# The sparse-attention step of a two-model kernel: its compression between the projection's blocks, scaled probabilities, and outputs by column halves

## The reference

```python
q, kc, vc, ks, vs, kw, vw, g = split(h @ w_in)      # 1024, six of 256, 48 columns
kcmp = silu((windows(rope(kc)) + pe) @ w1) @ w2       # 15 windows of 32 tokens, stride 16
vcmp = the same of vc
o_c = softmax(q @ kcmp) @ vcmp                       # compressed part, 15 keys a group
o_s = softmax(q @ ks) @ vs                           # all 4 blocks are chosen: causal
o_w = softmax(q @ kw) @ vw                           # window 512 > 256: causal
gates = sigmoid(g)
out = (gates[0] * o_c + gates[1] * o_s + gates[2] * o_w) @ w_out
```

## Time and profile before

| | |
|---|---|
| median of 3 runs | 2884.92 us (2884.88 to 2886.07) |
| profiled execution's own time | 2884.84 us |
| its span, first to last instruction | 2883.0 us |
| mean granted TensorE clock | 0.994 |
| PE / DVE / ACT / POOL busy | 98% / 65% / 54% / 5% of the span |
| the NSA step on PE | 1202.9 to 1374.6 us |

### The profile page before, as it was taken

The page is one execution under the profiler, slowest core; times in us unless marked ns, Lnnn a source line. Parts: engine busy times, 40 slices in busy tenths (PEclk is TensorE's granted clock), DMA queues, the critical chain, the costliest instruction groups (busy, mean ns, idle before and its releaser), DMA issues.

```text
span 2883.0 us, 34918 instructions
## 1 busy us (share of the span) xinstructions
PE 2812.2 (98%) x13484; PEld 2303.9 (80%) x13484; DVE 1860.1 (65%) x2728; ACT 1546.0 (54%) x2656; POOL 149.1 (5%) x254
## 2 busy tenths in 40 slices
PE   9999999999999999999999999999999999999998
PEld 7887788888788888878888888788787788787786
DVE  6766776676566677646776766677654754645654
ACT  6546654655665465546655546665444444444442
POOL 1010100000000000000001001100100000000000
PEclk9999999999999999999999999999999999999999
DMA  8664467566446766642566675367663665653652
GB/s 261 223 229 161 141 218 248 183 223 222 161 154 217 243 190 229 215 150 70 187 232 219 216 260 186 103 208 242 229 212 135 200 189 189 227 190 132 190 190 88
DMA packets 358629, 559.41 MB, mean 194 GB/s; under 512 B 14624, under 2 KB 246048, under 8 KB 358208
## 3 DMA queue, kind: packets, MB, share of 16 engines
q1 hardware_dynamic: 350720, 535.02, 55.8%
q0 software_dynamic: 7600, 21.81, 2.2%
q10 hardware_dynamic: 144, 0.36, 0.0%
HBM read 556.03 MB, written 1.10 MB: 193 GB/s over the span
## 4 chain that ended last, share of the span: by engine, by line
PE 92%; DVE 5%; ACT 1%; issue 1%; POOL 1%; DMA 0%; DVEq 0%; ACTq 0%; POOLq 0%
PE ps L660 38%; PE ps L721 26%; PE ps L666 19%; PE ps L630 4%; PE ps L832 1%; PE ps L801 1%; DVE LO L1508 1%; POOL ST L2046 1%; DVE XL L1549 0%; DVE M L1626 0%; PE ps L809 0%; DVE M L1587 0%; PE ps L949 0%; DVE SB L1791 0%; ACT SB L1326 0%
## 5 line engine op out<-in xcount | busy, mean ns | idle before, releaser
L660 PE MATMUL ps<-HI,XH 128*128 128x512 f32 (+1 forms) x2496 | 984.1, 394 | 4.0 <-DVE LO L1508 1.4
L660 PE MATMUL ps<-LO,XH 128*128 128x512 f32 (+1 forms) x2496 | 971.4, 389 | 0.0
L1508 DVE TENSOR_TENSOR LO<-RAW,HI 128x1024 fp32r<-128x1024 f32 x468 | 567.6, 1223 | 335.7 <-ACT HI L1169 332.9
L666 PE MATMUL ps<-HI,XL 128*128 128x512 f32 (+1 forms) x2496 | 769.4, 389 | 0.4
L1513 DVE SCALAR_TENSOR_TENSOR LO<-RAW,GC,HI 128x512 fp32r<-128x512 f32 (+1 forms) x896 | 622.4, 744 | 189.1 <-ACT HI L1176 186.6
L1169 ACT ACTIVATE HI<-RAW 128x1024 fp32r<-128x1024 f32 x468 | 490.5, 1059 | 457.6 <-PE ps L721 286.6
L1176 ACT ACTIVATE HI<-RAW,GC 128x512 fp32r<-128x512 f32 (+1 forms) x896 | 588.1, 714 | 158.0 <-PE ps L666 133.0
L666 PEld LDWEIGHTS ps<-HI,XL 128*128 128x128 f32 x2496 | 466.7, 188 | 105.7 <-DVE XL L1549 7.9
L660 PEld LDWEIGHTS ps<-HI,XH 128*128 128x128 f32 x2496 | 469.9, 188 | 101.2 <-issue 2.4
L660 PEld LDWEIGHTS ps<-LO,XH 128*128 128x128 f32 x2496 | 470.1, 188 | 92.6
L721 PE MATMUL ps<-HI,AH 128*128 128x512 f32 x880 | 273.5, 392 | 0.0
(11 more groups left out here) (182 smaller groups left out, 1968.7 us busy)
## 6 DMA issues: line engine op xcount, KB each, us to landing
RAW<-in_ffn_w_in SPq DMA_DIRECT2D x350, 512.0 KB, 4.7
RAW<-in_ffn_w_out SPq DMA_DIRECT2D x88, 1024.0 KB, 5.0
RAW<-in_w_ada SPq DMA_DIRECT2D x48, 1024.0 KB, 5.1
RAW<-in_w_in SPq DMA_DIRECT2D x44, 1024.0 KB, 5.1
RAW<-in_w_ffn_in SPq DMA_DIRECT2D x88, 512.0 KB, 4.7
RAW<-in_diff_w_in SPq DMA_DIRECT2D x24, 1024.0 KB, 5.1
RAW<-in_w_ffn_out SPq DMA_DIRECT2D x22, 1024.0 KB, 4.9
RAW<-in_moba_w_in SPq DMA_DIRECT2D x12, 1024.0 KB, 5.1
```

The lines of the kernel that those rows point to most:

```text
L660: e.matmul(ps[:, b + t, 0:nw], XH[:, k, t * P:(t + 1) * P], q[s][:, c * nw:(c + 1) * nw], start=(k == 0 and q is HI), stop=False)
L666: i = e.matmul(ps[:, b + t, 0:nw], XL[:, k, t * P:(t + 1) * P], HI[s][:, c * nw:(c + 1) * nw], start=False, stop=(k == 7))
L1508: e.tensor_tensor(LO[n % NSPLIT][:, 0:w], RAW[t.buf][:, at[1] * w:(at[1] + 1) * w], HI[n % NSPLIT][:, 0:w].bitcast(F32), ALU.subtract).the ...
```

## The change

The NSA step alone is rewritten; all others keep their code.

- The projection's blocks come in another order and cut: kc and vc, ks and vs, kw and vw, then the queries in two, each of 512 columns, and the gates' 48. The compression weights are loaded in two pairs of tiles, ahead of blocks 3 and 4.
- The compression runs between the blocks: its first half (`windows(0)`) behind block 2, its second behind block 3, hidden turn and second layer within block 4, the first scores too. The key turns are `doubled(0..3)`, of which two stand behind block 1, one behind block 2 and one in block 3 ahead of k2 = 2. `clock()` is gone. The small block writes to ps[4] and ps[5].
- The gates are made as exp(-x) on ACT, plus one and reciprocal on DVE, in place of a sigmoid.
- A unit is now a pair of heads with its two key sets in turn (units 2p and 2p + 1), and there is one more set of scores in flight ahead of the loop. The probabilities in SB are multiplied with CG, reciprocal sum times gate: one piece of 128 columns by DVE (`weights`), three pieces by POOL. The compressed probabilities are scaled too, in one DVE product.
- The turned heads are copied to PT by ACT (`first_head`) and DVE (`second_head`).
- `outputs_by_columns`: values are the weights, PT moves, and head j goes to partitions 64 j to 64 j + 63, so a pair's outputs stand turned, with rows by head, as XH and XL need them. The pair's two units and its compressed part (`compressed(p)`) add up in one bank; ACT and DVE take XH and XL from it (`pair_high`, `pair_low`). M, TP and `outputs_flipped` are not used here.
- Three of the output projection's halves are split at u = 9, 11 and 13. The last unit's outputs come behind the first row group of the projection.

Core of the diff (comment lines name the engine's queue; lines in brackets stand for several):

```diff
+NSA_BLOCKS = ((1024, 512), (1536, 512), (2048, 512), (0, 512), (512, 512), (2560, 48))
...
+            elif st.kind == "nsa":
+                for n, (c0, nw) in enumerate(NSA_BLOCKS):
+                    if n in (3, 4):
+                        tiles_windows(n - 3, st)
+                    tile_cols(a["nsa_w_in"][st.j], c0, nw, 0, st)
+                    tile_cols(a["nsa_w_in"][st.j], c0, nw, 1, st)
+                tile_rows(a["nsa_w_out"][st.j], st)
...
+            def outputs_by_columns(st, u, b, first, v):
+                PT = st.t["PT"]
+                for kt in range(2):
+                    for j in range(2):
+                        o = e.matmul(ps[64 * j:64 * j + 64, b, kt * P:S], v(kt),
+                                     PT[:, u % 2, j, 0:S] if kt == 0 else PT[:, u % 2, j, S:S + P],
+                                     start=(first and kt == 0), stop=False, skip_group_check=True)
+                o.then_inc(s_mix, 1)
...
 # TensorE
+                first_block(st, 512)
+                later_block(st, 1, 512)
+                doubled(0, 0)
+                doubled(1, 1)
+                later_block(st, 2, 512)
+                doubled(2, 0)
+                e.wait_ge(s_e, 8)
+                windows(0)
+                later_block(st, 3, 512, lambda k2: doubled(3, 1) if k2 == 2 else None)
+                windows(1)
+                later_block(st, 4, 512, in_queries)
+                e.wait_ge(s_tn, c["tn"] + 10)
+                later_block(st, 5, 48, None, 4)
+                e.wait_ge(s_cp, c["cp"] + 5)
+                unit_scores(1)
+                e.wait_ge(s_cp, c["cp"] + 6)
+                queries_turned(5)
+                e.wait_ge(s_ex, c["ex"] + 1)
+                unit_scores(2)
...
+                def in_queries(k2):
+                    if k2 == 1:
+                        hidden_turned()
+                    elif k2 == 2:
+                        queries_turned(4)
+                        compressed_made()
+                    elif k2 == 3:
+                        e.wait_ge(s_tn, c["tn"] + 10)
+                        e.wait_ge(s_cp, c["cp"] + 4)
+                        unit_scores(0)
...
-                e.wait_ge(s_vb, 4)
-                clock()
...
+                for u in range(17):
+                    if 1 <= u < 14:
+                        e.wait_ge(s_ex, c["ex"] + u + 1)
+                        unit_scores(u + 2)
+                    if u >= 1:
+                        turned(u - 1)
+                    if u >= 2:
+                        mixed(u - 2)
+                    if u in (2, 3):
+                        compressed_turned(u - 2)
...
+                def ready(k, t):
+                    if (k, t) == (0, 0):
+                        e.wait_ge(s_pt, c["pt"] + 15)
+                        e.wait_ge(s_p1, c["p1"] + 15)
+                        e.wait_ge(s_ol, c["ol"] + 4)
+                    elif (k, t) == (0, 1):
+                        e.wait_ge(s_ol, c["ol"] + 8)
...
 # ScalarE
+                block_out(0)
+                split(st.w0 + 13)
+                block_out(1)
+                turned_out(st, 0, XC[:, 0])
+                turned_out(st, 1, XC[:, 1])
+                split(st.w0 + 17)
+                block_out(2)
+                turned_out(st, 2, KSW[:, 0])
+                split(st.w0 + 20)
+                turned_out(st, 3, KSW[:, 1])
+                split(st.w0 + 21)
+                block_out(3)
+                split(st.w0 + 22)
+                for kv in range(2):
+                    at = slice(64 * kv, 64 * kv + 60)
+                    e.wait_ge(s_rawu, 3 + kv)
+                    e.activation(HS[at, :], ps[at, 6 + kv, 0:256], ACT.Silu).then_inc(s_hs, 1)
...
+                for u in range(3, 18):
+                    if u < 16:
+                        exps(st, u)
+                    first_head(u - 2)
...
+                    if u % 2 == 0 and u >= 6:
+                        pair_high(u // 2 - 3)
+                    if u in (9, 11, 13):
+                        split(st.w0 + 24 + (u - 7) // 2)
...
 # VectorE
+                rotated(0)
+                split(st.w0 + 13)
+                rotated(1)
+                split(st.w0 + 16)
+                e.wait_ge(s_nw, 96)
+                e.wait_ge(s_tn, c["tn"] + 4)
+                (the eight additions into E)
+                split(st.w0 + 17)
+                rotated(2)
+                split(st.w0 + 21)
+                rotated(3)
...
+                for u in range(2, 18):
+                    if u < 16:
+                        weights(u)
+                    if u == 2:
+                        (sums, reciprocal, gate, row mask, PC times CC)
+                    else:
+                        second_head(u - 2)
+                    if u + 2 < 16:
+                        maxima(st, u + 2)
+                    if u % 2 == 0 and u >= 6:
+                        pair_low(u // 2 - 3)
+                    if u in (9, 11, 13):
+                        split(st.w0 + 24 + (u - 7) // 2)
...
 # GpSimd
+                for u in range(16):
+                    e.wait_ge(s_cg, st.c["cg"] + u + 1)
+                    for j, t, c0, c1 in ((0, 1, 128, 384), (1, 0, 0, 128), (1, 1, 128, 384)):
+                        v = SB[:, u % 3, j, c0:c1]
+                        o = e.tensor_scalar(v, v, CG[:, u, t, j:j + 1], None, ALU.mult)
+                    o.then_inc(s_df, 1)
```

More of the change, by code:

```diff
@@ L701, in later_block @@
                 for k2 in range(4):
+                    if between is not None:
+                        between(k2)
                     w = st.w0 + 4 * n + k2
@@ L789, in turned_block, with scores @@
                 turn(ps[:, 5, :], srcs[4:]).then_inc(s_tb, 1)
[L791 to L793 removed]
+            def scores(st, i, q, k, decay=False, b=None):
+                b = 2 * (i % 2) if b is None else b
                 for j in range(2):
@@ new lines, in compressed_made @@
+                def compressed_made():
+                    e.wait_ge(s_nw, 96)
+                    e.wait_ge(s_hc, 1)
+                    for m in range(2):
+                        i = e.matmul(ps[:, 6, 0:60], W2D[:, m].rearrange("p u d -> p (u d)"), HK[:, m, :, 0:15],
+                                     start=(m == 0), stop=(m == 1))
+                    i.then_inc(s_kc, 1)
+                    e.wait_ge(s_hc, 3)
+                    for g in range(4):
+                        for m in range(2):
+                            i = e.matmul(ps[:, 7, g * 64:(g + 1) * 64], HV[:, m, g].rearrange("p u n -> p (u n)"),
+                                         W2[:, 1, m, :], start=(m == 0), stop=(m == 1))
+                    i.then_inc(s_vc, 1)
@@ L1041, in nsa, with compressed @@
-                mixed(15)
+                    elif u % 2 == 0 and p >= 2:
+                        e.wait_ge(s_ol, c["ol"] + p - 1)
+                    outputs_by_columns(st, u, 6 + p % 2, u % 2 == 0, value(u))
+                    if u == 2:
+                        compressed(0)
+                    elif u % 2 == 1 and p >= 1:
+                        compressed(p)
+                def compressed(p):
+                    if p == 0:
+                        e.wait_ge(s_vb, 4)
+                    for j in range(2):
+                        o = e.matmul(ps[64 * j:64 * j + 64, 6 + p % 2, 0:S], VB[:, p // 2, (2 * p + j) % 4, :],
+                                     PTC[:, p // 2:8:4, :], start=False, stop=True, skip_group_check=True)
+                    o.then_inc(s_co, 1)
@@ L1408, in nsa @@
                     e.wait_ge(s_rawu, 3 + kv)
-                    e.activation(HS[at, :], ps[at, kv, 0:256], ACT.Silu).then_inc(s_hs, 1)
+                    e.activation(HS[at, :], ps[at, 6 + kv, 0:256], ACT.Silu).then_inc(s_hs, 1)
                 e.wait_ge(s_z, 2)
@@ L1420, in nsa @@
                                          ).then_inc(s_hc, 1)
+                split(st.w0 + 23)
+                turned_out(st, 4, QT[:, 0:4, :])
                 e.wait_ge(s_kc, 1)
@@ L1442, in nsa @@
-                outputs_out(st)
+                split(st.w0 + 24)
+                block_out(4)
+                e.wait_ge(s_e, 8)
+                exps(st, 0)
+                block_out(5)
+                e.wait_ge(s_cp, c["cp"] + 6)
+                e.activation(GS[:, :, :, :].rearrange("p t h c -> p t (h c)"), TM[:, :, 2560:2608], ACT.Exp, scale=-1.0
+                             ).then_inc(s_gs, 1)
+                turned_out(st, 5, QT[:, 4:8, :])
+                exps(st, 1)
+                exps(st, 2)
@@ L1444, in mix2 @@
+                pair_high(6)
+                split(st.w0 + 30)
+                pair_high(7)
+                split(st.w1 + 2)
             def mix2(st):
@@ L1855, in nsa @@
                 pc = PC[:, :, :, 0:15]
-                for i in range(2):
-                    maxima(st, i)
                 e.wait_ge(s_vc, 1)
@@ L1861, in nsa @@
                                     cst("bmask").unsqueeze(2).to_broadcast([P, 4, 64]), ALU.mult).then_inc(s_vb, 1)
```

(11 more changed lines are left out.)

366 lines of the change are left out of this document (148 added, 218 removed).

## The result

The changed kernel takes 2911.64 us (median of 4 runs, 2910.8 to 2912.34) against 2884.9: ratio 1.0092 with an interval of 1.0074 to 1.0109, 26.7 us slower. The prediction had 2894.7, in a range of 2884 to 2903. Its direction was right, its size was not: +26.7 instead of +9.9. The profiled execution has a span of 2910.4 us and a mean granted clock of 0.989 (before 2883.0 and 0.994).

What follows compares the result with a forecast made beforehand. PE was taken to bound the kernel, at 92% of the chain. Ahead of the loop +20.7, loop -11.2 and output projection +0.4 made +9.9 us on 2884.84: 2894.7, range 2884 to 2903.

Steps and rivals of the forecast that it cites:

- Gaps (a) to (d): PE idle before block 1's doubled keys 5.2 us, before window matmuls 4.7, in block 3 9.6, in block 4 4.4.
- (c): Block 3: ScalarE's split waits for n = 16, its tile queued behind two loads waiting for PE; PE idles 9.6 us.
- (a): Before block 1's doubled keys: n = 12 lies in a later tile, issued at 1223.5; PE idles 5.2 us.
- (d): Block 4: a small tile waits for the second window half, then copies, table load and Silu; PE idles 4.4 us.
- (e): Behind each of the four gaps ahead of the loop PE's clock falls to half, 1.6 us each: +6.3.
- Rival 1: Clock stays full at the new gaps ahead of the loop: 6.3 us less, 2888.4; chance 0.13.
- (f): Projection blocks recut: the 48-column block takes 5.1 to 6.0 us, about +4; the slow stretch with `clock()` goes.
- Part 1: The pair loop: PE takes 2.75 us a unit, other engines follow; 44.7 us against 55.9, -11.2.
- Rival 4: In the loop PE runs empty entering column halves, 0.27 us instead of 0.05, 16 times: +3.5, 2898.2; chance 0.06.
- rival 2: GpSimd sets the loop, from 2.6 us for three scalings; at 2.9, +5.4, 2900.1; chance 0.11.
- Rival 3: Block 3's gap doesn't form because the tile with n = 16 is there in time: 2883.5; chance 0.12.
- Rival 5: The four gaps last half as long and a loop unit takes PE's bare 2.61 us: 2876; chance 0.06.

Runs made afterwards that it cites:

- run 1: Changed kernel with ScalarE's split ahead of block 2's copy ending one half earlier, so it doesn't wait for n = 16: 2899.94 us.
- run 2: Changed kernel with both pairs of compression weights loaded behind block 3's tiles: 2897.62 us.
- run 7: Changed kernel with the edits of run 1, run 2 and run 3, and VectorE's eight position additions ahead of its split up to n = 15: 2882.60 us.
- run 8: Run 7 with a last projection block of 256 columns, 48 of them used, instead of 48: 2882.13 us.
- run 10: Run 9 with the compression's hidden units turned on PE one quarter block later: 2877.02 us.
- run 11: Run 10 with a last projection block of 256 columns instead of 48: 2876.07 us.
- run 4: Changed kernel with a last projection block of 256 columns, 48 of them copied out, instead of 48: 2912.79 us.
- run 3: Changed kernel with a pair's XH and XL taken one unit earlier and the three loop splits moved one iteration: 2907.93 us.
- run 5: Changed kernel with one of GpSimd's three scalings of a unit left out, so part of the computation is missing: 2911.26 us.
- run 9: Run 7 with two output projection splits in the loop's tail (u = 14, 16) instead of three among its maxima: 2880.97 us.

## Why the prediction was wrong, step by step

The sum had two wrong terms: the loop, -11.2 forecast and -2.2 measured (53.7 for 55.9), and the way to it, +20.7 forecast and +28.1 measured. The steps behind them, one by one:

- **What bounds it.** Right: PE sets the end, and everything lost or won was PE's waits or its clock.
- **Gaps (a) to (d).** All formed, together 22.67 us for 23.9. (c) was named with its queues and measured at 10.34 for 9.6; runs 1 and 2 show its cause. (a) was short by 1.0. The step that failed in it is "1223.5 now as the shorter rotation frees 0.3": I weighed GpSimd beside DVE for the loop and not for the splits beside the four copies, which sent the load out 1.5 us late. That the copies cause it is read from rows, and no run tried it apart. (d) was over by 2.3: its 96 KB landed in 2.5 us rather than 3.0, and the table load of 1.3 ahead of Silu isn't taken (the trace has none there; in the profile before one stands ahead of the sigmoid and one ahead of Silu, and the sigmoid is an exponential now, behind Silu; that this is why is read from the two traces).
- **(e), the clock behind gaps.** 7.3 us for 6.3. Rival 1 falls.
- **(f), the small block, and the start of the loop.** Failed: "5.1 to 6.0" was 7.8. I priced the matmuls of 48 columns by a pitch at full clock, and took the slow stretch before the old loop as something that goes with `clock()`. It stayed in another form: 8.5 us lost in the small block, the scores, the turns and the first units. The reading was wrong already in the profile before. There the clock falls at 1287.7, 1.9 us ahead of the first matmul of `clock()` (1289.61), within the narrow compressed scores:

```profile
1285.16 4.64 PE L991 MATMUL ps<-KC,QT 128*128 128x32 f32 x32
```

  In the profiles of runs 7 and 8, and of 10 and 11, which differ in the last block alone, the clock falls in or right behind the block of 48 columns and stays full through one of 256 and the scores behind it. That narrow matmuls bring the fall is shown so far; it isn't a rule for each of them. Run 10's block itself kept the clock, runs 4 and 8 lost 1.7 us each at the 32-column scores in spite of the wide block, and run 11 lost nothing there.
- **Part 1, the unit of 2.75 us (3.47 measured).** Failed in the step "Do the other engines follow at 2.75?". I summed each engine's busy time, and DVE's 2.3 was less than 2.75. What sets the unit is the order in DVE's queue: XL behind maxima that wait for the next masks (3.87 us in four waits; run 3 takes 3.7 off). Two further waits for PT behind the splits are 1.05, so "its slack of 0.4 per unit takes part" was right in kind: the splits cost PE 1.05 in the middle and 1.7 in its last unit. PE's own work is 3.08 us with a compressed part (forecast 2.97) and 2.67 without (5.75 - 3.08; forecast 2.54). Six of the ten units have one, so PE alone has 29.2 for 27.5.
- **GpSimd.** 2.50 us for three scalings against 1.8: the value was wrong, its range (1.2 to 2.9) held, and rival 2's point of 2.6 was nearly reached. Run 5 shows that it isn't the bound at 3.44 a unit, and in run 3's pairs of 5.75 us, 2.88 a unit, PE has no wait for it either.
- **Rival 4, emptying at switches.** Entering the column halves costs about 0.08 us (from the turns' start to the outputs' 0.67 in the earlier trace rows, 0.75 here), not 0.27. The Trainium skill (TensorEngine Tiling (Array Packing), section Tiling Modes, Key Properties) says that a change of tiling mode drains TensorE. The trace shows no such price: a unit with a compressed part takes 3.08 us where the bare sum is 2.83, and these 0.25, 0.11 over the forecast, are all that its three changes can have cost.
- **Output projection.** 24.44 for 24.3. Right.
- **Rival 3, (c) doesn't form: 2883.5.** It was to decide at the load's 10.1 us; 9.9 was measured. Its time was wrong too: without (c) the kernel took 2899.94, since the other failed terms remain.
- **Rival 5** (shorter gaps, a unit of 2.61) falls with both: the gaps are 22.67 us, the unit 3.47.
- **Range.** Its upper end of 2903 is already more than its named parts give (2900.1 + 0.9 + 0.8 = 2901.8), and no part of it allowed for half clock in and behind the small block or for waits by the order of VectorE's queue in the loop.

## What to carry to other kernels

A sum of busy times says that an engine could follow; whether it does is in the order of its queue: write down for each wait of the bounding engine what stands ahead of its releaser. A tile that PE itself reads holds its buffer until PE has used it, and in a strict load queue everything behind it waits as well; place it by when its buffer is freed, not by when it is wanted. When waits are taken away one after another, expect their prices to add only until the next engine is late: the last 5 us of clock bought 1 us at most.

## What the hardware showed beyond that

- TensorE's clock fell from 2.4 to 1.2 GHz with no idle time before it, in a run of matmuls of 48 columns (runs 7, 9 and after), and in run 10 right behind such a run; a block of 256 columns in its place kept it at 2.4 (runs 4, 8 and 11).
- VectorE's two-input split of 128x512 took 1.095 us beside a GpSimd copy and 0.736 alone.
- GpSimd's scaling by one value a partition took 0.6 us for 128 columns (2.50 - 1.91) and 0.96 for 256 (1.91 / 2).
- A change between row halves, full array and column halves of the array cost PE about 0.1 us or less each (0.08 into the column halves, 0.75 for 0.67).
